# Norms in halves of 256 tokens around a two-block float32 transformer kernel

## The chip, the cores and the metric

The kernel runs on one core of a Trainium2 chip. The metric is the device time of one execution in microseconds, as a median of runs; lower is better. A profile is one execution taken by the hardware profiler. Engines in the profile: PE is TensorE (matmul), PEld its weight loads, DVE is VectorE, ACT is ScalarE, POOL is GpSimd, SP is SyncE, which issues all large transfers.

## The reference

Two transformer blocks run one after the other over 512 tokens of width 1024. What matters here is the order of norms and projections:

```
block 1: u = rmsnorm(h, norm1_w) * (1 + sc1) + sh1;  proj = u @ w_in           # w_in: 28 tiles of 128 columns
         o_hg = hgrn2(...);  o_da = diff_attention(...)
         h = h + g1 * (concat(o_hg, o_da) @ w_out)                             # out1
         u = rmsnorm(h, norm2_w) * (1 + sc2) + sh2                             # norm 1
         h = h + g2 * ((silu(u @ w_gate) * (u @ w_up)) @ w_down)               # ff1, down1
         h = rmsnorm(h, final_norm_w)
block 2: u = rmsnorm(h, ...) * (1 + sc1) + sh1                                 # norm 2
         proj = u @ w_in_2;  kc, vc = compress(k_cmp), compress(v_cmp)         # kc2, qa2, compress, kv2
         sparse attention, stick-breaking attention, gated merge
         h = h + g1 * (merged @ w_out_2)                                       # out2
         u = rmsnorm(h, ...) * (1 + sc2) + sh2                                 # norm 3
         h = h + g2 * ((silu(u @ w_gate_2) * (u @ w_up_2)) @ w_down_2)         # ff2, down2
out = rmsnorm(h, final_norm_w_2)                                               # norm 4
rmsnorm(x, w) = x * rsqrt(mean(x * x) + eps) * w;   mod = silu(c) @ w_ada + b_ada gives the sh, sc, g
compress(k) = gelu((blocks(k) + pos_emb) @ w1) @ w2
```

The final norm of block 1 and norm 2 are computed from one sum over the tokens; a second sum (of raw squares, `ssr`) scales the residual itself later.

## The kernel before

Everything lies transposed: channels on the 128 partitions, tokens along the free axis. `res` holds the residual as 8 tiles of 128 channels x 512 tokens. The weights come as units, one 128-column tile of a weight matrix each (512 KB where all 8 blocks of 128 rows are in it). `plan()` numbers all units of the program in order; `ph.u0` is the first of a phase. SyncE loads a unit into one of two slots of `wraw` as soon as the unit two before it has been split. VectorE splits it (`split`): `wh` is the value rounded for the fast matmul format, `wl` the rest. TensorE then does for each block k three matmuls, `wh` with the high and the low part of the input and `wl` with the high part (`passes`), 24 for a unit, into one bank of 128x512. In-order queues on each engine and counting semaphores set the order: `w_hi` and `w_split` count split units, `unit_done` finished ones, `drain_a` and `drain_v` banks read by ScalarE and VectorE.

A norm goes like this. VectorE adds the bank of each output tile, times its gate, to `res`; ScalarE squares it into `sq`; GpSimd adds up seven of the eight squares in `ssq`. TensorE multiplies `ssq` and the last square with ones to sum over the partitions (`norm`); ScalarE takes the root, VectorE the reciprocal, TensorE spreads it over the partitions with four transposes (`spread`). Then for each of the 8 tiles VectorE makes `tn` (L1705), ScalarE rounds it to `uh` (L1225) and VectorE makes the rest `ul` (L1710). TensorE starts the first two units of the next phase tile by tile as `ul` comes (`passes_both`, L640 to L642). The third unit is split by VectorE only when one of these two is finished. out1a (first half of w_out's rows, 8 units of 4 blocks) leaves tiles 3 to 7 in five banks, and out1 (second half, 8 more units) accumulates onto them.

Behind norm 2, TensorE does kc2 (2 units), then the sums of `ssr` (L991, signals `r_sum`), then the first two units of qa2, the spread of that second root (`r_rstd`), then compress: for n = 0, 1 sixteen matmuls (L1001) and one with `wfin` (L1006), which waits for `c_pos`. GpSimd computes `wfin` from the compress weights in `wpos`, which lies over `ssr`; it waits for `r_sum` ahead of that:

```
g.wait_ge(n_ul, KT * 3)
g.wait_ge(r_sum, 1)
g.wait_ge(c_in, 64)
... wpos[:] = w1c[:, n] * vt2[...]; four folding additions     # L581, L586, each signals c_pos
```

ScalarE drains each of kc2's two banks with four copies (L1446, L1447), and qa2's first unit waits for the first bank (`drain_a`). Norm 4 ends the program: VectorE and ScalarE scale four rows of `outb`, and SyncE stores each.

## Time and profile before

| | us |
|---|---|
| median of 3 runs (lowest, highest) | 1540.92 (1538.4, 1542.06) |
| the profiled execution's own time | 1538.91 |
| its span, first to last instruction | 1537.2 |
| TensorE busy in it | 1463.1 |
| VectorE, ScalarE, GpSimd busy | 986.6, 423.2, 95.5 |

The busy time of TensorE holds each matmul's way through the array, so two neighbours overlap in it; the spacing of starts says how fast a stream runs. "Idle before" in brackets gives the wait ahead of a row and what ended it. The granted clock is a share of full speed.

### The profile page before, as it was taken

How to read it: one execution, taken by the hardware profiler on the slowest of the kernel's cores; microseconds unless marked ns; L12 is line 12 of the kernel's file. 1: busy time of each engine (PE TensorE's matmuls, PEld its weight loads, DVE VectorE, ACT ScalarE, POOL GpSimd, SP SyncE). 2: the span in 40 equal slices, each digit the busy share in tenths (PEclk: the TensorE clock that was granted, in tenths of full speed). 3: DMA queues.
4: the chain of work that ended last, by engine and by line, in shares of the span. 5: the costliest groups of instructions: out<-in, count | busy, mean ns of one | idle time of the engine just before them, and what ended most of it. 6: DMA issues, size and time to landing. Idle time of an engine off the chain costs nothing.

```text
span 1537.2 us, 19550 instructions
## 1 busy us (share of the span) xinstructions
PE 1463.1 (95%) x7186; PEld 1170.1 (76%) x7186; DVE 986.6 (64%) x1727; ACT 423.2 (28%) x901; POOL 95.5 (6%) x75
## 2 busy tenths in 40 slices
PE   3989999889999999998999999999998999999997
PEld 2777876667888888887876666778886888888886
DVE  8789888886767666556556666775546444444343
ACT  5333354432110110003234445531113221221011
POOL 0100000020000000222600000000030000000110
PEclk9999999999999999998999999999998999999999
DMA  9243232344556565543221111113331323233322
GB/s 374 80 156 110 69 138 77 96 144 153 192 195 193 194 195 157 153 126 121 73 69 42 48 50 42 49 49 109 96 110 55 109 84 107 92 99 89 103 86 93
DMA packets 52611, 175.80 MB, mean 114 GB/s; under 512 B 5953, under 2 KB 6337, under 8 KB 52545
## 3 DMA queue, kind: packets, MB, share of 16 engines
q1 hardware_dynamic: 52544, 174.94, 35.1%
q8 instruction: 39, 0.64, 0.2%
q14 instruction: 28, 0.22, 0.0%
HBM read 172.82 MB, written 2.10 MB: 114 GB/s over the span
## 4 chain that ended last, share of the span: by engine, by line
PE 51%; ACT 1%; DVE 1%; issue 0%; ACTq 0%; DVEq 0%
PE bank L628 11%; PE bank L630 11%; PE bank L629 11%; PE bank L1070 8%; PE bank L1089 2%; PE bank L1124 2%; PE bank L1101 2%; PE bank L640 1%; PE bank L641 1%; PE bank L642 1%; PE bank L1001 0%; DVE wl L1611 0%; PE bank L1114 0%; PE bank L1045 0%; PE bank L737 0%
## 5 line engine op out<-in xcount | busy, mean ns | idle before, releaser
L628 PE MATMUL bank<-uh,wh 128*128 128x512 f32 x808 | 316.0, 391 | 6.0 <-DVE wl L1611 4.8
L630 PE MATMUL bank<-uh,wl 128*128 128x512 f32 x808 | 315.1, 390 | 0.0
L629 PE MATMUL bank<-ul,wh 128*128 128x512 f32 x808 | 315.0, 390 | 0.0
L1609 DVE CAST wh<-wraw 128x1024 fp32r<-128x1024 f32 (+1 forms) x235 | 156.2, 665 | 196.8 <-PE bank L630 180.0
L1611 DVE TENSOR_TENSOR wl<-wraw,wh 128x1024 fp32r<-128x1024 f32 (+1 forms) x235 | 275.1, 1171 | 8.1
L628 PEld LDWEIGHTS bank<-uh,wh 128*128 128x128 f32 x808 | 152.1, 188 | 39.0 <-issue 4.9
L630 PEld LDWEIGHTS bank<-uh,wl 128*128 128x128 f32 x808 | 151.9, 188 | 31.9
L629 PEld LDWEIGHTS bank<-ul,wh 128*128 128x128 f32 x808 | 152.1, 188 | 31.4
L628 PE MATMUL bank<-hh,wh 128*128 128x512 f32 x352 | 137.5, 391 | 0.0
L630 PE MATMUL bank<-hh,wl 128*128 128x512 f32 x352 | 137.1, 389 | 0.0
L629 PE MATMUL bank<-hl,wh 128*128 128x512 f32 x352 | 137.0, 389 | 0.0
L1631 DVE CUSTOM_DVE_ANT_0 ada<-ada,scb,vt 128x1024 f32<-128x1024 f32 x80 | 104.8, 1331 | 0.0
L1269 ACT ACTIVATE hh<-hf 128x512 f32 x44 | 27.8, 633 | 246.9 <-DVE hf L1727 246.9
L1727 DVE TENSOR_TENSOR hf<-sg,bank 128x512 f32<-128x512 f32 x44 | 30.2, 688 | 96.8 <-PE bank L630 96.8
L539 POOL TENSOR_TENSOR ssq<-sq 128x512 f32<-128x512 f32 x4 | 7.9, 1978 | 1185.9 <-ACT sq L1208 1185.9
L630 PEld LDWEIGHTS bank<-hh,wl 128*128 128x128 f32 x352 | 66.1, 188 | 13.9
L629 PEld LDWEIGHTS bank<-hl,wh 128*128 128x128 f32 x352 | 66.1, 188 | 13.7
L628 PEld LDWEIGHTS bank<-hh,wh 128*128 128x128 f32 x352 | 66.1, 188 | 13.4
L1070 PE MATMUL bank<-uh,wh 128*128 128x512 f32 x160 | 67.5, 422 | 2.2 <-ACT kdup L1473 2.2
L1070 PE MATMUL bank<-ul,wh 128*128 128x512 f32 x160 | 66.0, 412 | 0.0
L1267 ACT ACTIVATE sg<-bank 128x512 f32<-128x512 f32 x44 | 26.4, 601 | 143.1 <-PE bank L630 137.4
L1070 PE MATMUL bank<-uh,wl 128*128 128x512 f32 x160 | 64.5, 403 | 0.0
(355 smaller groups left out, 2331.6 us busy)
## 6 DMA issues: line engine op xcount, KB each, us to landing
ada<-in_w_ada_dram SPq DMA_DIRECT2D x96, 512.0 KB, 4.6
wraw<-in_w_in_dram SPq DMA_DIRECT2D x61, 512.0 KB, 3.4
wraw<-in_w_ffn_gate_dram SPq DMA_DIRECT2D x44, 512.0 KB, 3.3
wraw<-in_w_ffn_up_dram SPq DMA_DIRECT2D x44, 512.0 KB, 3.3
wraw<-in_w_ffn_down_dram SPq DMA_DIRECT2D x32, 512.0 KB, 3.5
wraw<-in_w_ffn_down_dram SPq DMA_DIRECT2D x16, 384.0 KB, 3.1
wraw<-in_w_out_dram SPq DMA_DIRECT2D x16, 256.0 KB, 2.8
wraw<-in_w_out_dram SPq DMA_DIRECT2D x8, 512.0 KB, 3.4
```

What stands on the lines that cost most here:

```text
L628: nc.tensor.matmul(bank[:], a, rh[:, k0 + k, :], start=(first and k == 0), stop=False)
L629: nc.tensor.matmul(bank[:], a, rl[:, k0 + k, :], start=False, stop=False)
L630: mm = nc.tensor.matmul(bank[:], b, rh[:, k0 + k, :], start=False, stop=(last and k == nk - 1))
L1070: mm = nc.tensor.matmul(B[1][:], (wl if p == 2 else wh)[:, slot, k * P:(k + 1) * P], (ul if p == 1 else uh)[:, k, :], start=(k == 0 and p ...
L1089: mm = nc.tensor.matmul(B[4 + 2 * (m % 2) + ab][:, 0:ZLEN[i]], q[:, i * P:(i + 1) * P], k[:, 0:ZLEN[i]], start=True, stop=True)
L1101: mm = nc.tensor.transpose(B[2 + ab][:, j * P:(j + 1) * P], zt[2 * (m % 3) + ab][:, j * P:(j + 1) * P], ident[:])
L1124: mm = nc.tensor.matmul(B[0][64 * ab:64 * ab + 64, i * P:(i + 1) * P], v, wt2[2 * (m % 2) + ab][:, j * P:(j + 1) * P], start=(first and br ...
L1269: A(hh[:, ds(i, 1), :].rearrange("p a t -> p (a t)"), hf[:, 0], ACT.Copy).then_inc(hh_ok, 1)
L1609: V.tensor_copy(wh[:, slot, 0:n], wraw[:, slot, 0:n]).then_inc(w_hi, 1)
L1611: V.tensor_tensor(wl[:, slot, 0:n], wraw[:, slot, 0:n], wh[:, slot, 0:n].bitcast(F32), ALU.subtract).then_inc(w_split, 1)
L1631: V.tensor_tensor_reduce(ada[:, slot, :], ada[:, slot, :], scb[:, m, :], 1.0, vt[:, t:t + 1], ALU.mult, ALU.add, modt[:, t:t + 1]).then_in ...
L1727: V.tensor_tensor(hf[:, 0], sg[:, 0], B[1][:], ALU.mult).then_inc(h_ok, 1)
```

## The change

The tokens are cut into two halves (`HALVES`) where a norm is near. The last tiles of a projection (from 4 on in out1, 6 and 7 in out2, 7 in down1 and down2) are computed first for 256 tokens, then for the other 256, into two banks; adds, squares, sums, root, spread and the norm's three operations run for each half. VectorE itself adds the last whole square and the first half's squares of norm 1, and one of norm 3. out1 loads its weights as 4 units with two tiles each, and its tiles 4 to 7 no longer accumulate onto out1a's banks; VectorE adds those to `res` by themselves. The two units behind a norm are split into buffers of their own (`XH`), and the third one is rounded by ScalarE (`ahead_cast`) and its rest made by VectorE behind the first tile of the norm (`open_rest`). The modulations of down1 come at other units, the last at the 18th of 24. The sums of `ssr`, with the signal `r_sum`, stand behind qa2's first two units, and the spread that belongs to them behind compress. The final stage scales and stores rows 0, 1 with the first half and rows 2, 3 with the second.

```diff
+        SPLIT_FROM = {1: 4, 2: 7, 3: 6, 4: 7}
+        PARTS = {k: [(t, None) for t in range(m)] + [(t, h) for h in range(2) for t in range(m, KT)]
+                 for k, m in SPLIT_FROM.items()}
+        SQUARED, ADDED, ADDS = {}, {}, {}
+        for k_ in PARTS:
+            for t_, h_ in PARTS[k_]:
+                SQUARED[k_, t_, h_] = len(SQUARED) + 1
+                if 0 < t_ < KT - 1:
+                    ADDED[k_, t_, h_] = len(ADDED) + 1
+            ADDS[k_] = len(ADDED)
+        ADDED_V = {(1, 3, None), (1, 4, 0), (1, 5, 0), (1, 6, 0), (3, 6, 0)}
...
+            def piece(bank, cc, slot, w0, nk, rh, rl, k0, first, last):
+                for k in range(nk):
+                    a = wh[:, slot, (w0 + k) * P:(w0 + k + 1) * P]
+                    b = wl[:, slot, (w0 + k) * P:(w0 + k + 1) * P]
+                    nc.tensor.matmul(bank[:, cc], a, rh[:, k0 + k, cc], start=(first and k == 0), stop=False)
+                    nc.tensor.matmul(bank[:, cc], a, rl[:, k0 + k, cc], start=False, stop=False)
+                    mm = nc.tensor.matmul(bank[:, cc], b, rh[:, k0 + k, cc], start=False, stop=(last and k == nk - 1))
+                return mm
...
+            def behind_norm(ph, nu):
+                hi, lo = XH[ph.name]
+                for h, cc in enumerate(HALVES):
+                    for k in range(KT):
+                        if h == 0 and k == 2:
+                            norm_sums(nu, 1)
+                        if h == 0 and k == 6:
+                            spread_half(nu, 1)
+                        pe.wait_ge(n_ul, N_UL[nu] + KT * h + k + 1)
+                        for c, bank in enumerate(OPEN[ph.name]):
+                            a = hi[:, c, k * P:(k + 1) * P]
+                            b = lo[:, c, k * P:(k + 1) * P]
+                            nc.tensor.matmul(bank[:, cc], a, uh[:, k, cc], start=(k == 0), stop=False)
+                            nc.tensor.matmul(bank[:, cc], a, ul[:, k, cc], start=False, stop=False)
+                            mm = nc.tensor.matmul(bank[:, cc], b, uh[:, k, cc], start=False, stop=(k == KT - 1))
+                            if h and k == KT - 1:
+                                mm.then_inc(unit_done, 1)
...
+                i = ph.iters - 1
+                for t in range(2):
+                    take(ph, i, t)
+                    pe.wait_ge(drain_v, ph.d0 + 2 * i + t - 1)
+                    piece(OUT2_HALF[0][t], HALVES[0], (ph.u0 + t) % 2, 0, KT, rh, rl, 0, True, True).then_inc(tile_ok, 1)
+                piece(OUT2_HALF[1][0], HALVES[1], ph.u0 % 2, 0, NT, rh, rl, 0, True, False)
+                norm_sums(3, 0)
+                piece(OUT2_HALF[1][0], HALVES[1], ph.u0 % 2, NT, NT, rh, rl, NT, False, True).then_inc(unit_done, 1)
+                spread_half(3, 0)
+                piece(OUT2_HALF[1][1], HALVES[1], (ph.u0 + 1) % 2, 0, KT, rh, rl, 0, True, True).then_inc(unit_done, 1)
...
+                slots = [(ph.u0 + 3 + c) % 2 for c in range(3)]
+                take(ph, last, 3)
+                (a0, b0), (a1, b1), (a2, b2) = DOWN
+                bank, other = DOWN_HALF[name]
+                piece(bank, HALVES[0], slots[0], 0, b0 - a0, hh, hl, a0, True, False)
+                piece(other, HALVES[1], slots[0], 0, b0 - a0, hh, hl, a0, True, False).then_inc(unit_done, 1)
+                if tiles_out:
+                    turn_out(KT - 2)
+                take(ph, last, 4)
+                piece(bank, HALVES[0], slots[1], 0, b1 - a1, hh, hl, a1, False, False)
+                take(ph, last, 5)
+                piece(bank, HALVES[0], slots[2], 0, b2 - a2, hh, hl, a2, False, True).then_inc(tile_ok, 1)
+                piece(other, HALVES[1], slots[1], 0, NT, hh, hl, a1, False, False)
+                norm_sums(4 if tiles_out else 2, 0)
+                piece(other, HALVES[1], slots[1], NT, NT, hh, hl, a1 + NT, False, False).then_inc(unit_done, 1)
+                if tiles_out:
+                    turn_last(0)
+                else:
+                    spread_half(2, 0)
+                piece(other, HALVES[1], slots[2], 0, b2 - a2, hh, hl, a2, False, True).then_inc(unit_done, 1)
...
+            def norm_sums(k, h):
+                pe.wait_ge(ssq_ok, added(k, KT - 2, h))
+                if h:
+                    pe.wait_ge(sq_ok, squared(k, KT - 1, h))
+                for j in (2 * h, 2 * h + 1):
+                    nc.tensor.matmul(SUMS[k][:, j:j + 1], ssq[:, j * P:(j + 1) * P], ones[:, 0:1], start=(j == 2 * h),
                                      stop=False, skip_group_check=True)
-                pe.wait_ge(sq_ok, KT * k)
-                for j in range(NT):
-                    mm = nc.tensor.matmul(B[4][:, j:j + 1], sq[:, 1, j * P:(j + 1) * P], ones[:, 0:1], start=False,
-                                          stop=(j == NT - 1), skip_group_check=True)
+                pe.wait_ge(sq_ok, squared(k, KT - 1, h))
+                for j in (2 * h, 2 * h + 1):
+                    mm = nc.tensor.matmul(SUMS[k][:, j:j + 1], sq[:, 1, j * P:(j + 1) * P], ones[:, 0:1], start=False,
+                                          stop=(j == 2 * h + 1), skip_group_check=True)
                 mm.then_inc(n_sum, 1)
+            def spread_half(k, h):
+                pe.wait_ge(n_col, 2 * (k - 1) + h + 1)
+                for j in (2 * h, 2 * h + 1):
+                    mm = nc.tensor.transpose(SPREAD[k][h][:, j * P:(j + 1) * P], rcol[:, j:j + 1].broadcast_to([P, P]),
+                                             ident[:])
+                mm.then_inc(n_rstd, 1)
...
+            for h, cc in enumerate(HALVES):
+                for t in range(4, KT):
+                    slot, w0 = take(ph, 0, t // 2), NT * (t % 2)
+                    if h:
+                        pe.wait_ge(part_ok, t - 3)
+                    else:
+                        pe.wait_ge(drain_v, ph.d0 + t - 3)
+                    mm = piece(OUT1_HALF[h][t - 4], cc, slot, w0, NT, mixh, mixl, NT, True, True)
+                    mm.then_inc(unit_done if h and t % 2 else tile_ok, 1)
+                    if h and t == 4:
+                        norm_sums(1, 0)
+                    if h and t == 5:
+                        spread_half(1, 0)
+            ffn("ff1", 1, H1)
             down("down1", 0)
-            norm(2)
-            spread(B[7], rcol, n_col, 2, n_rstd)
-            simple("kc2", uh, ul, 2 * KT)
+            ph = PH["kc2"]
+            take(ph, 0, 1)
+            pe.wait_ge(drain_a, ph.a0)
+            behind_norm(ph, 2)
...
+            simple("qa2", uh, ul, part=(0, 1))
             pe.wait_ge(ssr_ok, 7)
             for j in range(NT):
                 mm = nc.tensor.matmul(B[6][:, j:j + 1], ssr[:, j * P:(j + 1) * P], ones[:, 0:1], start=(j == 0),
                                       stop=(j == NT - 1), skip_group_check=True)
             mm.then_inc(r_sum, 1)
-            simple("qa2", uh, ul, part=(0, 1))
-            spread(B[6], rcolr, r_col, 1, r_rstd)
 
...
+            spread(B[6], rcolr, r_col, 1, r_rstd)
...
+            def ahead_cast(ph):
+                u = ph.u0 + 2
+                act.wait_ge(w_in[u % 2], 16 * (u // 2 + 1 - FRONT // 2))
+                act.wait_ge(unit_done, u - 3 + U1)
+                act.wait_ge(w_split, u)
+                A(wh[:, u % 2, :], wraw[:, u % 2, :], ACT.Copy).then_inc(w_hi, 1)
...
+            def through_norm(nu, name, late, shift, bias=epst, scale=None, then=None):
+                ph = {1: PH["ff1"], 2: PH["kc2"], 3: PH["ff2"]}[nu]
+                norm_std(nu, 0, bias)
+                ahead_cast(ph)
                 for t in range(KT):
-                    act.wait_ge(n_t, KT * (nu - 1) + t + 1)
-                    A(uh[:, t, :], tn[:, t % 4], ACT.Identity, bias=shift[:, t:t + 1]).then_inc(n_uh, 1)
+                    norm_u(nu, shift, t, 0)
+                    if t >= 1 and t - 1 < len(late):
+                        part_square(name, nu, late[t - 1], 1, scale)
+                    if t == 3 + len(late):
+                        norm_std(nu, 1, bias)
+                for t in range(KT):
+                    norm_u(nu, shift, t, 1)
...
+            def split_open(ph, c):
+                u = ph.u0 + c
+                slot, (hi, lo) = u % 2, XH[ph.name]
+                v.wait_ge(w_in[slot], 16 * (u // 2 + 1 - FRONT // 2))
+                V.tensor_copy(hi[:, c, :], wraw[:, slot, :]).then_inc(w_hi, 1)
+                v.wait_ge(w_hi, u + 1)
+                V.tensor_tensor(lo[:, c, :], wraw[:, slot, :], hi[:, c, :].bitcast(F32),
+                                ALU.subtract).then_inc(w_split, 1)
...
+            def open_rest(ph):
+                u = ph.u0 + 2
+                v.wait_ge(w_hi, u + 1)
+                V.tensor_tensor(wl[:, u % 2, :], wraw[:, u % 2, :], wh[:, u % 2, :].bitcast(F32),
+                                ALU.subtract).then_inc(w_split, 1)
...
+            def through_norm(nu, shift, late):
+                ph = {1: PH["ff1"], 2: PH["kc2"], 3: PH["ff2"]}[nu]
+                for h in range(2):
+                    for t in range(KT + 1):
+                        if t < KT:
+                            norm_in(nu, t, h)
+                        if t:
+                            norm_low(nu, shift, t - 1, h)
+                        if h == 0 and t == 1:
+                            open_rest(ph)
+                        if h == 0 and 1 <= t <= len(late):
+                            late[t - 1]()
+                        if h == 0 and t == len(late) + 4:
+                            norm_rstd(nu, 1)
...
+            def add_out1a(t):
+                v.wait_ge(unit_done, PH["out1a"].u0 + t + 1 + U1)
+                V.scalar_tensor_tensor(res[:, t, :], (B[1] if t < 3 else OUT1_BANKS[t])[:], mod1[:, 16 + t:17 + t], res[:, t, :],
+                                       op0=ALU.mult, op1=ALU.add).then_inc(drain_v if t < 3 else part_ok, 1)
+            def add_out1(t, h=None):
+                n = {None: t, 0: t, 1: t + 4}[h]
+                ph = PH["out1"]
+                if h == 0:
+                    v.wait_ge(part_ok, t - 3)
+                if t % 2 and h != 0:
+                    v.wait_ge(unit_done, ph.u0 + t // 2 + 1 + U1)
+                else:
+                    v.wait_ge(tile_ok, {0: 1, 2: 2, 4: 3, 5: 4, 6: 5, 7: 6, 8: 7, 10: 8}[n])
+                add_part(OUT1_BANKS[t] if h is None else OUT1_HALF[h][t - 4], t, h, mod1[:, 16:24])
...
+            ph, fu = PH["out1"], PH["ff1"]
+            split(ph.u0 + 1, (ph.u0 + 1) % 2)
+            add_out1(0)
+            for t in (4, 5):
+                add_out1a(t)
+            add_out1(1)
+            split(ph.u0 + 2, ph.u0 % 2)
+            for t in (6, 7):
+                add_out1a(t)
+            add_out1(2)
+            split(ph.u0 + 3, (ph.u0 + 1) % 2)
+            add_out1(3)
+            add_square(1, 3)
+            split_open(fu, 0)
+            for t in range(4, KT):
+                add_out1(t, 0)
+                if t > 4:
+                    add_square(1, t - 1, 0)
+            add_out1(4, 1)
+            v.wait_ge(mod_done, 40)
+            gains(1, mod1, vt1, NORM_B, 32)
+            split_open(fu, 1)
+            norm_rstd(1, 0)
+            through_norm(1, mod1[:, 24:32], [lambda t=t: add_out1(t, 1) for t in (5, 6, 7)])
```

## Rows read from the trace of the kernel before

**Rows 1.** the page, busy us, share of the span and instructions of TensorE.
```profile
PE 1463.1 (95%) x7186; PEld 1170.1 (76%) x7186; DVE 986.6 (64%) x1727; ACT 423.2 (28%) x901; POOL 95.5 (6%) x75
```

**Rows 2.** stretches around the norms: length, busy (x) of PE, PEld, DVE, ACT, POOL; PEclk, DMA, GB/s.
```profile
311.00:334.40 23.40, 22.50 (x96) 17.79 (x96) 20.87 (x33) 4.72 (x8) 8.16 (x6) 1.00 0.58 180
334.40:341.30 6.90, 2.74 (x21) 2.27 (x20) 5.30 (x9) 2.37 (x5) 1.20 (x1) 0.81 0.48 152
341.30:354.30 13.00, 12.95 (x48) 10.39 (x48) 8.97 (x14) 7.15 (x9) 0.00 (x0) 0.84 0.00 0
354.30:362.40 8.10, 5.98 (x26) 4.48 (x25) 7.23 (x11) 1.37 (x3) 0.00 (x0) 1.00 0.58 190
705.20:713.20 8.00, 3.66 (x22) 3.10 (x20) 6.32 (x10) 2.89 (x5) 1.63 (x1) 0.64 0.42 130
713.20:726.20 13.00, 13.00 (x48) 10.56 (x49) 8.87 (x14) 4.80 (x7) 0.00 (x0) 0.83 0.43 154
1152.30:1160.00 7.70, 3.71 (x21) 3.11 (x19) 5.00 (x8) 2.27 (x4) 0.00 (x0) 0.64 0.26 85
1160.00:1173.20 13.20, 13.15 (x48) 10.55 (x48) 8.96 (x14) 6.08 (x8) 0.00 (x0) 0.82 0.00 0
```

**Rows 3.** TensorE, groups by line (busy, mean ns), then its timeline (start, duration).
```profile
L817 PE MATMUL bank<-ql,kl 128*128 128x128 f32 x224 | 30.7, 281 | 2.9 <-DVE kl L1899 2.8
...
195.36 1.05 PE L817 MATMUL bank<-ql,kl 128*128 128x128 f32 x8
```

**Rows 4.** VectorE, groups by line, then one row of its timeline.
```profile
L1611 DVE TENSOR_TENSOR wl<-wraw,wh 128x1024 fp32r<-128x1024 f32 x203 | 251.9, 1241 | 7.0
...
L1631 DVE CUSTOM_DVE_ANT_0 ada<-ada,scb,vt 128x1024 f32<-128x1024 f32 x80 | 104.8, 1331 | 0.0
...
L1705 DVE SCALAR_TENSOR_TENSOR tn<-res,gain,bank 128x512 f32<-128x512 f32 x24 | 17.5, 741 | 3.3 <-PE bank L745 2.1 <-issue 1.3
...
L1899 DVE TENSOR_TENSOR kl<-p,xx 128x256 f32<-128x256 f32 x28 | 11.7, 417 | 0.0
...
318.74 2.31 DVE L1631 CUSTOM_DVE_ANT_0 ada<-ada,scb,vt 128x1024 f32<-128x1024 f32 x1
```

**Rows 5.** ScalarE, timeline behind norm 1 and behind kc2.
```profile
349.24 1.28 ACT L1434 ACT_TABLE_LOAD   x1
350.54 1.06 ACT L1434 ACTIVATE scb<-scb 128x1024 f32<-128x1024 f32 x1
...
725.75 0.59 ACT L1446 ACTIVATE kds<-bank 64x512 f32<-64x512 f32 x1 [4.71 <-PE bank L642]
```

**Rows 6.** GpSimd, timeline of the compress weights.
```profile
727.31 3.93 POOL L581 TENSOR_TENSOR wpos<-w1c,vt 128x2048 f32<-128x2048 f32 x1 [18.16 <-PE bank L991]
...
737.16 0.46 POOL L586 TENSOR_TENSOR wfin<-wpos 128x128 f32<-128x128 f32 x1
...
747.18 0.46 POOL L586 TENSOR_TENSOR wfin<-wpos 128x128 f32<-128x128 f32 x1
```

**Rows 7.** TensorE, timeline from kc2 to qa2's third unit.
```profile
726.23 0.94 PE L991 MATMUL bank<-ones,ssr 128*128 128x1 f32 x8
728.29 0.47 PE L628 MATMUL bank<-uh,wh 128*128 128x512 f32 x1 [1.12 <-ACT kds L1447]
...
735.18 0.50 PE L628 MATMUL bank<-uh,wh 128*128 128x512 f32 x1 [1.20 <-DVE wl L1611]
...
741.23 3.71 PE L1001 MATMUL bank<-kds,w1c 128*128 128x62 f32 x32
...
748.56 0.32 PE L1006 MATMUL bank<-ones,wfin 128*128 128x1 f32 x2
```

**Rows 8.** timeline of the last tile and of the tail.
```profile
1520.22 0.39 PE L629 MATMUL bank<-hl,wh 128*128 128x512 f32 x1
...
1525.89 0.39 PE L630 MATMUL bank<-hh,wl 128*128 128x512 f32 x1
...
1531.58 0.35 ACT L1593 ACTIVATE outb<-bank,tiny 128x128 f32<-128x128 f32 x1
```

423 lines of the change are left out of this document (230 added, 193 removed).

## The prediction

> **What bounds the kernel now.** I read the page's busy shares first, then the waits of TensorE, then its timeline wherever it idles, and last the stretches by engine. TensorE is busy 95% of the span [rows 1], so time can be won only where it idles or crawls. Three such places are alike: the norms behind out1, down1 and out2. TensorE issues its last projection, then for 6.9, 8.0 and 7.7 us does only the sums and the spread of 1/std, and then its 48 matmuls of the first two tiles take 13.0, 13.0 and 13.2 us instead of 48 x 0.227 = 10.9, since part of them runs at the lower clock level: the granted clock averages 0.84, 0.83 and 0.82 [rows 2]; the 0.227 is the spacing of the matmuls at 1520.22 and 1525.89, 25 places apart [rows 8]. Behind the first norm the third tile also waits for VectorE. These are what the change aims at. The fourth place is the tail, 11.3 us from the last matmul to the end of the span [rows 8]. A fifth row matters for what the change moves: GpSimd's work on the compress weights, which today is just hidden [rows 6, 7].
>
> **The price of halves.** A pair of weight load and 256-column matmul is not in this trace. The nearest row is L817: eight pairs, each a 128x128 load and a matmul of 128 columns in plain float32, take 1.05 us, the last one's own 0.281 included, so (1.05 - 0.281)/7 = 0.110 apart [rows 3]. From above: a whole one of 512 columns costs 0.227; if what is not columns (0.227 - 512/2.4 GHz = 0.014) is fixed, a half costs 0.107 + 0.014 = 0.120. I take 0.117, so a whole in two halves costs 0.007 more; ends 0.110 and 0.120, and 0.125 if loads interfere. VectorE: a TENSOR_TENSOR falls from 1.241 us at 1024 columns to 0.417 at 256, 0.275 per 256 columns [rows 4]. So the norm's instruction of 0.741 (spaced 0.66, each starts 0.08 before its forerunner ends) becomes 0.47, spaced 0.41 (an estimate, from these rows; 0.33 if it scaled fully, 0.45 with more overhead). 32 of them take 13.1 us instead of 16 x 0.66 = 10.6. TensorE consumes a half tile for two weight tiles in 6 x 0.117 = 0.70 while VectorE makes it in 0.82: behind each norm VectorE sets the pace.
>
> Row L817 says 0.110 per pair. The Trainium skill (TensorE: Matmul & The Clock Gate, "Back-to-back issue gap") gives 262 cycles for N = 256, that is 109 ns when warm. It gives 216 ns for N = 512, where this trace has 227, so I don't take it; by it the halves would win about 3 us over my sum, which speaks for rival 2.
>
> **out1 and norm 1.** VectorE is busy 20.9 of 23.4 us there already [rows 2]. Added on it: four adds of out1a's tiles 4 to 7 into res (they used to stay in PSUM) 4 x 0.66 = 2.6; eight half adds for four whole +0.6; one whole and three half additions of squares +1.6. Four wide splits for eight narrow ones give back 1.0. Going through its new order from 311.0 (first split 0.8 longer, then splits 3 x 1.9, three modulations 3.8, adds 7.9, squares 2.3 with the wait for ScalarE, both opening splits 3.8, the small ones 0.5), the reciprocal of the first half comes at about 335.8. Sums and spread for that half cost 0.9 more, then 13.1 for the halves, 1.15 for the rest of the third tile, 1.2 for three late half adds, 0.9 for the second reciprocal and waits where a half begins: 353.0. TensorE meanwhile stands about 3 us before the first sums, and that costs nothing, since VectorE is the late one. Collisions with GpSimd: a modulation of 1.33 took 2.31 beside a GpSimd add [rows 4]; I take 1.2, between 0 and 2.5. So the last low half is there at 354.2. Next is late: ScalarE loads its table (1.28), does the Silu of the second condition vector (1.06) and the first Silu of the FFN (some 0.6, as its copies) [rows 5], and the third tile's matmuls wait for that: 356.7. Before, TensorE issued 26 matmuls in the 8.1 us up to 362.4, which are 5.9 us of work [rows 2]: 2.2 lost by waits for the split tiles, 1.7 of it ahead of the third tile (start 356.0) and the rest a tile later, so its effective start is 356.8. Change: 0 (from -2 to +2).
>
> The row at 318.74 shows the slowing [rows 4]. The skill (SBUF — State Buffer, "Who interferes with whom") says VectorE with two SBUF inputs and GpSimd hold a shared port pair exclusively, for whole instructions. By it the squares moved from GpSimd to VectorE save VectorE up to 1 us each time; that is inside my bounds.
>
> **down1 and norm 2, up to compress.** I count from the start of down1's last tile: 705.22 - 66 x 0.227 = 690.2. Its first half is complete after 90 halves, 10.5. Behind it VectorE adds (0.2 later, 0.47), ScalarE squares, TensorE has 12 halves as cover and sums at 12.0 to 12.9; std and reciprocal come under the next 12 halves; spread at 14.5; first norm instruction at 14.8; ScalarE's cast of the third tile (1.04) delays the first high half by 0.3; then 13.1 + 1.15 + 0.4 (late add) + 1.3 (reciprocal; the second half's spread stands behind k = 5 on TensorE and is about 0.6 late): last low half 30.8, kc2 complete at 31.6. Before it was 726.2 - 690.2 = 36.0. qa2's first unit waits, as before [rows 7], for the four copies of kc2's first bank, 4 x 0.59 [rows 5], with the raw square now ahead of them: starts at 34.0 instead of 38.1. A gain of 4.1.
>
> Then comes the step that I think decides. GpSimd multiplies and folds the compress weights: it starts when r_sum has been signalled (727.31, right behind L991 at 726.23) and ends its first result at 737.6 (737.16 and its 0.46), its second at 747.6 [rows 6, 7]: 11.4 and 21.4 us after the sums begin. TensorE waits for these (c_pos) inside compress. Before, qa2's two units stood between the r_sum matmuls and compress, and the second wait was met with one microsecond to spare (748.56 against 747.64). The change puts the r_sum matmuls behind qa2's units, right ahead of compress. GpSimd's wait on r_sum is unchanged, and so is its chain. Now nothing but 2 x 3.6 us of compress matmuls lies beside 20.3 us of GpSimd. With R the start of the r_sum matmuls: matmuls of n = 0 until R + 4.6, wait until R + 11.4 (6.8 us idle), n = 1 until about R + 15 to 18.5, wait until R + 21.4. Without the waits it is R + 8.7: a stall of 12.8 (12 to 13.5; GpSimd's second round had VectorE beside it and took as long as the first, so it won't shorten much). Behind such a gap TensorE starts at its lower level, and the norms lost 2.1 us by that; I add 2.0. Queued behind the wait on TensorE: the spread for raw_rows and qa2's last two units; VectorE waits with them for c_h.
> R = 34.0 + 2 x 5.44 = 44.9; the second c_h at 66.4, spread 0.4: qa2's third unit at 66.8. Before: 748.8 - 690.2 = 58.6, its stall of 1.2 [rows 7] included. With the slow clock: a loss of 10.2; rounded with VectorE's uncertain spacing 10.4. Tables on GpSimd shift too, but stand to TensorE as before, counted from R.
>
> **out2 and norm 3.** From the start of tile 6, 1152.3 - 2 x 5.44 = 1141.4. Both first halves are done at 5.7; VectorE comes to them at 4.8 behind two splits, adds and squares until 6.9; sums at 7.1 to 8.1; spread 9.8; first norm instruction 10.1; then 0.6 for the cast, 13.1, 1.15, 0.8 (two late adds) and 0.9: 26.6; matmuls end at 27.4, before 31.8. The third tile is rounded already, so it starts at about 28.1, behind table load and Silu; before, it waited for the split as behind norm 1, 1.7 us, 33.5. A gain of 5.4, with 1 us either way.
>
> **down2 and the tail.** 66 wholes in halves +0.5; sums and transposes of the first half now lie in TensorE's stream, with the turn of tile 6 before them, +1.6. The tail behind 1525.9, in which ScalarE scales the last row until 1531.9 [rows 8], shortens: add -0.27, square and the copy behind it -0.8, two rows instead of four to scale -1.0, half the bytes to store perhaps -0.3. Sum -0.3, taken as 0 (-1 to +1.5).
>
> **Sum.** 0 + 10.4 - 5.4 + 0 = +5.0 on the profiled execution's 1538.9 (span 1537.2 and 1.7 around it): 1543.9. That execution lies 2.0 below the median of the runs; on the median it is 1545.9, predicted 1546.
>
> **Rivals.**
> 1. The stall at compress isn't there, because GpSimd gets done ahead of TensorE after all. Without the 12.8 and the 2.0 the sum is -9.8: 1531. For it: the norms do shorten in the way the rows say. Against it: the wait on r_sum still stands in GpSimd's queue and its rows have no slack. It decides from the point where GpSimd's start no longer follows qa2. Chance 0.10; the other side.
> 2. Halves cost 0.110 and norm 1 wins its 2 us: some 320 halves are not under VectorE's pace, 320 x 0.007 = 2.2, together -4.2: 1541.7, no change. For it row L817, against it that the type there is another. 0.16.
> 3. The lower clock level comes on also in the halved norms, as TensorE waits about 1 us again and again for VectorE. A half tile then takes 6 x 0.213 = 1.28 and not 0.70, above VectorE's 0.82; for 4 us at each norm that is about 1.5 us, three times: +4.5, 1550.4. For it: the granted clock of 0.64 in two of the gaps [rows 2]. Against: the new gaps are far shorter. 0.12.
> Forecast as summed: 0.62.
>
> **Numbers.** A change of 0.2% (3.1 us) is about what can be told from none. The forecast's own spread is 3.5 us, 1542.5 to 1549.5. Slower: nearly all of the forecast and rival 3, 0.72. Same: rival 2 and the low edge of the forecast, 0.18. Faster: 0.10. The range, with rival 2's lower values and rival 3: 1539.5 to 1551.5.
>
> **What would show it.** Right: in the waits of TensorE, the matmul with wfin (L1006 before) waits for GpSimd twice, about 6.8 and 3 to 6 us; kc2's matmuls end about 4 us earlier against down1; ff2's third tile starts without waiting for wl. 256-column matmuls 0.110 to 0.125 apart. The norm's VectorE instructions spaced 0.41. Wrong: no wait for GpSimd in compress; halves above 0.15 apart; a clock below 1.0 through the halved norms; norm 1 more than 2 us off either way.

## The result

The changed kernel takes 1547.58 us in the median (1546.08 to 1550.08, 5 runs), the kernel before 1540.92 (1538.4 to 1542.06, 5 runs beside them): the ratio is 1.0047, with a 95% interval of 1.0037 to 1.0058. Predicted were 1546 and slower. The profiled execution has a span of 1543.7 us, against 1537.2; it was the fastest of the five, with a time of 1546.08 us, so 2.4 us of its time lie outside the span, where the kernel before has 1.7.

The page's busy line of the changed kernel, beside [rows 1]: TensorE is busy 7.2 us longer and idle no longer in sum than before (73.4 us, before 74.1). The new waits behind norm 2 are not to be seen here, since the norms have given up as much idle time elsewhere, and slow matmuls count as busy. The stretches between fixed points show the loss.

```profile
PE 1470.3 (95%) x7558; PEld 1194.7 (77%) x7558; DVE 993.3 (64%) x1786; ACT 408.3 (26%) x919; POOL 89.6 (6%) x74
```

I laid the two traces side by side at seven fixed points of TensorE's timeline. Each number is the length of one stretch in us:

| stretch | before | after | difference | predicted |
|---|---|---|---|---|
| start to the end of a wait for the attention's weights (287.89, 289.23) | 287.9 | 289.2 | +1.3 | 0 |
| to the start of down1's last tile | 402.4 | 405.5 | +3.1 | 0 |
| to qa2's third unit | 58.5 | 66.7 | +8.2 | +8.2 |
| to out2's tile 6 | 392.7 | 392.0 | -0.7 | +2.0 |
| to the third unit of the second FFN | 33.5 | 28.0 | -5.5 | -5.4 |
| to down2's last tile | 336.1 | 336.1 | 0 | 0 |
| to the end of the span | 26.2 | 26.2 | 0 | 0 |

The first row has nothing to do with the change: that point lay between 287.9 and 289.8 in the profiled executions of all kernels of this study, before any changed instruction. Each stretch is read from one execution of each kernel, so a difference of one or two us can also be scatter.

The wait that I had named as the deciding one. TensorE's waits in the changed kernel (us in total, times, longest), and then its timeline (start, duration) from the r_sum matmuls (now L1122, before L991) to qa2's third unit, which answers to [rows 7]:

```profile
PE bank L1135 <- POOL wfin L636: 6.5, 2, 5.2
```
```profile
741.54 0.95 PE L1122 MATMUL bank<-ones,ssr 128*128 128x1 f32 x8
742.35 3.79 PE L1130 MATMUL bank<-kds,w1c 128*128 128x62 f32 x32
751.38 0.59 PE L1135 MATMUL bank<-ones,wfin 128*128 128x1 f32 x2 [5.24 <-POOL wfin L636]
751.83 7.07 PE L1130 MATMUL bank<-kds,w1c 128*128 128x62 f32 x32
760.18 0.59 PE L1135 MATMUL bank<-ones,wfin 128*128 128x1 f32 x2 [1.28 <-POOL wfin L636]
760.63 1.09 PE L859 MATMUL bank<-ident,tiny 128*128 128x128 f32 x4
761.37 0.78 PE L678 MATMUL bank<-uh,wh 128*128 128x512 f32 x1
```

The same 32 matmuls of 62 columns take 3.79 us ahead of the first wait and 7.07 behind it. The granted clock was 1.00 from 742.35 to 747.00 and 0.50 from 751.83 to 760.00, the lower of the two levels, so it fell in the gap; and the second round was slow enough to hide most of the second wait. GpSimd's timeline of the same stretch, which answers to [rows 6]:

```profile
742.62 3.61 POOL L631 TENSOR_TENSOR wpos<-w1c,vt 128x2048 f32<-128x2048 f32 x1 [14.01 <-PE bank L1122]
746.31 4.48 POOL L636 TENSOR_TENSOR wpos<-wpos 128x1024 f32<-128x1024 f32 x3
750.87 0.46 POOL L636 TENSOR_TENSOR wfin<-wpos 128x128 f32<-128x128 f32 x1
...
759.67 0.45 POOL L636 TENSOR_TENSOR wfin<-wpos 128x128 f32<-128x128 f32 x1
```

Its round takes 8.7 us, where [rows 6] show 10.3 and 10.0: VectorE has nothing to do meanwhile. Its first instruction has 14.01 us of idle time before it, and in brackets stands what it waited for: TensorE's L1122.

The stretches of the changed kernel around the norms (length, busy (x) of PE, PEld, DVE, ACT, POOL, then PEclk, DMA, GB/s), beside [rows 2]:

```profile
312.00:336.66 24.66, 19.18 (x110) 16.37 (x108) 23.70 (x35) 4.99 (x10) 4.43 (x2) 1.00 0.54 170
336.66:344.80 8.14, 8.14 (x43) 8.14 (x43) 5.77 (x11) 2.60 (x6) 0.72 (x1) 0.58 0.20 67
344.80:361.35 16.55, 14.13 (x113) 13.47 (x111) 15.04 (x37) 11.17 (x21) 1.69 (x2) 1.00 0.12 36
...
741.50:761.37 19.87, 13.35 (x81) 12.95 (x81) 1.15 (x6) 2.46 (x5) 17.81 (x13) 0.71 0.00 0
...
1160.00:1181.39 21.39, 20.19 (x161) 19.34 (x161) 17.61 (x41) 12.57 (x25) 0.80 (x1) 1.00 0.24 75
```

Ahead of the first norm VectorE is busy 23.70 of 24.66 us, and the 8 us behind run at the lower level (0.58). At the third norm nothing of the kind is seen: the granted clock is 1.00 throughout, against 0.64 and 0.82 in [rows 2].

### The profile page after: what moved, and what is told of

Its sections match the earlier page's. It is cut to its first block, busy times and chain, and to the rows that moved or that the text cites. A ratio compares the mean times of both kernels' runs of the same rounds, so it can differ in the third digit from the quotient of the medians.

```text
span 1543.7 us, 20402 instructions
## 1 busy us (share of the span) xinstructions
PE 1470.3 (95%) x7558; PEld 1194.7 (77%) x7558; DVE 993.3 (64%) x1786; ACT 408.3 (26%) x919; POOL 89.6 (6%) x74
## 4 chain that ended last, share of the span: by engine, by line
PE 85%; DVE 8%; ACT 3%; issue 2%; POOL 1%; DMA 0%; DVEq 0%; SPq 0%; ACTq 0%; POOLq 0%
PE bank L678 18%; PE bank L680 18%; PE bank L679 18%; PE bank L1200 8%; PE bank L1219 2%; PE bank L1254 2%; PE bank L931 2%; PE bank L1231 2%; PE bank L903 1%; PE bank L905 1%; PE bank L904 1%; PE bank L1041 1%; DVE ada L1795 1%; PE bank L688 1%; PE bank L876 1%
## 5 line engine op out<-in xcount | busy, mean ns | idle before, releaser
L1759 DVE CAST wh<-wraw 128x1024 fp32r<-128x1024 f32 (+1 forms) x222 | 148.3, 668 | 183.1 <-PE bank L680 170.3
L1761 DVE TENSOR_TENSOR wl<-wraw,wh 128x1024 fp32r<-128x1024 f32 (+1 forms) x222 | 259.3, 1168 | 7.6
L678 PE MATMUL bank<-hh,wh 128*128 128x512 f32 x308 | 120.3, 391 | 0.0
L680 PE MATMUL bank<-hh,wl 128*128 128x512 f32 x308 | 119.9, 389 | 0.0
L679 PE MATMUL bank<-hl,wh 128*128 128x512 f32 x308 | 119.9, 389 | 0.0
L1423 ACT ACTIVATE hh<-hf 128x512 f32 (+1 forms) x44 | 27.8, 632 | 240.9 <-DVE hf L1930 240.9
L680 PEld LDWEIGHTS bank<-hh,wl 128*128 128x128 f32 x308 | 57.8, 188 | 12.0
L679 PEld LDWEIGHTS bank<-hl,wh 128*128 128x128 f32 x308 | 57.8, 188 | 11.9
L678 PEld LDWEIGHTS bank<-hh,wh 128*128 128x128 f32 x308 | 57.8, 188 | 11.9
## 6 DMA issues: line engine op xcount, KB each, us to landing
fraw<-in_w_in_dram SPq DMA_DIRECT2D x6, 512.0 KB, 14.8
```

Source lines behind the costliest of these rows:

```text
L678: nc.tensor.matmul(bank[:], a, rh[:, k0 + k, :], start=(first and k == 0), stop=False)
L679: nc.tensor.matmul(bank[:], a, rl[:, k0 + k, :], start=False, stop=False)
L680: mm = nc.tensor.matmul(bank[:], b, rh[:, k0 + k, :], start=False, stop=(last and k == nk - 1))
L1759: V.tensor_copy(wh[:, slot, 0:n], wraw[:, slot, 0:n]).then_inc(w_hi, 1)
L1761: V.tensor_tensor(wl[:, slot, 0:n], wraw[:, slot, 0:n], wh[:, slot, 0:n].bitcast(F32), ALU.subtract).then_inc(w_split, 1)
```

## The experiments

All were timed against the kernel before on the same chip; it had medians of 1540.3, 1541.0 and 1540.9 us in the three groups of runs. Line numbers of the variants are shifted against the changed kernel's where lines came or went.

**1. The order of r_sum alone, taken back.**

```diff
+            (r_sum matmuls, signal r_sum)
             simple("qa2", uh, ul, part=(0, 1))
-            (r_sum matmuls, signal r_sum)
             (compress)
```

> The changed kernel with one block moved back: the four r_sum matmuls stand again right behind kc2's tiles, ahead of the first two units of qa2. Theory (the wait for GpSimd inside compress is the loss): GpSimd starts its two rounds of 8.7 us at about 729.7 instead of 742.6 and is done at 738.4 and 747.2, and TensorE comes to the two matmuls with wfin at about 745.3 and 749, so it waits for neither; the 6.5 us of waits, the slow matmuls of the second round and the slow clock behind it go, 12.6 us in all: 1547.6 - 12.6 = 1535.0, and 1533 to 1537. Rival (what comes behind compress, the rows rescaled by VectorE or the copies of ScalarE, holds qa2's third unit anyway): the wait shows up under another name, 1545 to 1548.

Measured: 1534.62 us (1533.65 to 1537.81), ratio 0.9963 (0.9950 to 0.9975). TensorE's timeline at the second wait:

```profile
749.36 0.38 PE L1135 MATMUL bank<-ones,wfin 128*128 128x1 f32 x2 [0.25 <-POOL wfin L636]
749.61 0.63 PE L859 MATMUL bank<-ident,tiny 128*128 128x128 f32 x4
750.00 0.47 PE L678 MATMUL bank<-uh,wh 128*128 128x512 f32 x1
```

6.5 us of waits became 0.25, the third unit starts at 750.00 and not at 761.37, and the time falls by 13.0 us in the median, against 12.6 expected. (The two profiled spans lie 10.6 apart: that of the changed kernel was the fastest of its five executions, that of experiment 1 the second slowest.) The rival falls: nothing behind compress held it. GpSimd began at 729.93 as expected; its first round took 10.6 us, not 8.7, since VectorE was busy beside it, and that still fitted.

**2. The same order put into the kernel before, all norms whole.**

```diff
-            (r_sum matmuls)
             simple("qa2", uh, ul, part=(0, 1))
-            spread(B[6], rcolr, r_col, 1, r_rstd)
+            (r_sum matmuls)
             (compress)
+            spread(B[6], rcolr, r_col, 1, r_rstd)
```

> The kernel before with the reverse edit alone: the r_sum matmuls behind qa2's first two units, and with them, as in the changed kernel, the root on ScalarE, the reciprocal on VectorE, the spread behind compress and the first two rescaled rows. All norms whole. Theory: from r_sum to qa2's third unit 19.8 us as in the changed kernel, where the kernel before has r_sum at 727.3 and the third unit at 748.7: r_sum at 739.2, third unit at 759.0, plus 1.1 of slow clock: 1540.9 + 11.4 = 1552.3, and 1550 to 1554. Rival (the loss is of the halves and not of this order): 1540 to 1543.

Measured: 1555.14 us (1552.77 to 1555.55), ratio 1.0088 (1.0075 to 1.0101), 14.8 over the kernel before. Its timeline:

```profile
742.37 0.95 PE L992 MATMUL bank<-ones,ssr 128*128 128x1 f32 x8
743.18 3.79 PE L1000 MATMUL bank<-kds,w1c 128*128 128x62 f32 x32
752.21 0.59 PE L1005 MATMUL bank<-ones,wfin 128*128 128x1 f32 x2 [5.23 <-POOL wfin L586]
752.66 7.07 PE L1000 MATMUL bank<-kds,w1c 128*128 128x62 f32 x32
761.01 0.58 PE L1005 MATMUL bank<-ones,wfin 128*128 128x1 f32 x2 [1.29 <-POOL wfin L586]
761.46 1.10 PE L745 MATMUL bank<-ident,tiny 128*128 128x128 f32 x4
762.20 0.78 PE L628 MATMUL bank<-uh,wh 128*128 128x512 f32 x1
```

The pattern is the changed kernel's row by row, 19.8 us from r_sum to the third unit, with no norm halved. The order alone makes a kernel slower than the whole change does. It came out 2.8 above my number and above my range. In its profiled execution the stretch from down1's last tile to qa2's third unit is 10.4 us longer than in the kernel before, as worked out (10.3). What is over lies elsewhere: 1.6 us ahead of everything changed, 1.4 in the first norm, untouched, and 3.1 between qa2's third unit and out2's tile 6, where the matmuls ran at the lower clock level longer: about 1.5 right behind the compress gap (1.1 expected) and 1.5 behind the 64 matmuls of 32 columns that follow later (L1045). Stretches there, for the kernel before, the changed one and this one (columns as above):

```profile
774.00:778.00 4.00, 4.00 (x30) 3.35 (x29) 2.63 (x4) 0.00 (x0) 0.00 (x0) 0.70 0.01 2
```
```profile
790.00:794.00 4.00, 4.00 (x19) 3.33 (x18) 3.90 (x5) 1.06 (x1) 0.00 (x0) 1.00 0.00 0
```
```profile
792.00:796.00 4.00, 4.00 (x10) 3.09 (x10) 3.90 (x5) 1.06 (x1) 0.00 (x0) 0.50 0.01 2
```

Which of this comes in every execution and which is scatter of single ones, no run shows.

**3 and 4. The first norm and out1 whole again**, on the changed kernel, and on experiment 1's.

```diff
-        Phase("out1", 1, 4, 0, 8, 4)
+        Phase("out1", 1, 8, 0, 8)
-        SPLIT_FROM = {1: 4, 2: 7, 3: 6, 4: 7}
+        SPLIT_FROM = {1: 8, 2: 7, 3: 6, 4: 7}
...
+                        if nu == 1:
+                            passes_both((B[0], B[1]), slots, uh, ul)
```

> The changed kernel with out1 and the first norm as in the kernel before: eight half units of out1, out1a's tiles 4 to 7 left in PSUM, all squares of this norm added by GpSimd, one reciprocal and one spread, whole instructions, the first two tiles of the FFN in the ring's slots. The norms behind down1, out2 and down2 stay in halves. Theory from the two traces (the first norm in halves lost 3.2 us: the third unit starts 75.4 us behind a fixed gap in TensorE's work and not 72.1): 1547.6 - 3.2 = 1544.4. My prediction (net 0 here): 1547.6. Below 1543 the halves of out1 cost more than the traces show.

> Both edits together: r_sum ahead of qa2 and the first norm whole. If the two losses are independent: 1547.6 - 12.6 - 3.2 = 1531.8. If the time won at the first norm is given back before compress (by the weights' loads or by a wait for VectorE), 1535, as with r_sum alone.

Measured: 1545.32 us (1542.02 to 1546.61), ratio 1.0031 (1.0020 to 1.0042); and 1531.35 us (1526.87 to 1532.72), ratio 0.9932 (0.9919 to 0.9945). The first of these came 0.9 above the expected 1544.4. So halving the first norm costs 2.3 us by the first pair of medians and 3.3 by the second; the intervals of the first pair overlap, those of the second don't. From the attention's wait to the third unit of the FFN the traces have 72.1 us in the changed kernel, 72.2 in experiment 1, and 69.0 and 68.3 with the norm whole (68.1 in the kernel before). Over all profiled executions of the study this stretch took 70.9 to 73.8 us with the first norm in halves and 68.1 to 69.7 with it whole. The two losses add up as expected in experiment 4 (1531.8). The fourth kernel, that of experiment 4, is 9 us under the kernel before: the change without its first norm and with r_sum where it was. Only experiment 6, a variant of it, is as fast.

Not all of that cost lies in the norm. With the first norm in halves, the tail behind the start of down2's last tile takes 26.2 us (26.5 in experiment 9), and with it whole but the rest changed 25.5, although the tail's program is the same; the last store is issued 0.36 us behind the end of the issue before it, and not 0.04. And outside the span lie 1.7 to 1.9 us of the time in every execution of the kernels with the first norm whole, but 1.7 to 4.0, 2.4 in the median, in those with it in halves. So about 1.3 us of the 2.3 to 3.3 come at the end of the program or outside the span; what causes them no run shows.

**5. Squares of the first norm back on GpSimd**, on experiment 1's kernel.

```diff
-        ADDED_V = {(1, 3, None), (1, 4, 0), (1, 5, 0), (1, 6, 0), (3, 6, 0)}
+        ADDED_V = {(3, 6, 0)}
```

> The changed kernel with r_sum ahead of qa2 (1534.6), and with the first norm's four additions of squares that VectorE had taken (one of 512 columns, three of 256) given back to GpSimd; all else in halves as it is. Theory (the first norm loses because VectorE is the late engine ahead of its first reciprocal): these four take 0.69 + 3 x 0.41 = 1.9 us of VectorE; GpSimd's own last half addition of 0.7 to 0.85 then stands in the chain instead of 0.41, so about 1 us is won: 1533.6. Rival (GpSimd's additions slow VectorE's instructions beside them as much as they relieve it, by 1 us for each whole one): 1534.6 to 1536.

Measured: 1536.85 us (1535.13 to 1540.74), ratio 0.9975 (0.9964 to 0.9987). The theory missed: slower by 2.2 and not faster by 1, and a little above the rival's range too. The intervals of this run and of experiment 1 overlap, so the size is uncertain; in the traces the norm takes 73.8 us and 72.2. The first sums of the norm wait for GpSimd, longer than they waited for VectorE (2.81):

```profile
337.63 0.60 PE L839 MATMUL bank<-ones,ssq 128*128 128x1 f32 x4 [3.56 <-POOL ssq L589]
```

So taking these additions to VectorE seems to have paid in the change, although VectorE is the busy engine there.

**6. The spread of the second half behind k = 3**, on the fourth kernel, at the norm behind down1.

```diff
-                        if h == 0 and k == 6:
+                        if h == 0 and k == (4 if nu == 2 else 6):
                             spread_half(nu, 1)
```

> The kernel with r_sum ahead of qa2 and the first norm whole (1531.35), and the spread of the second half's 1/std behind k = 3 of the first half's tiles instead of behind k = 5, at the norm behind down1 alone. Theory: the reciprocal is there 3.6 us before TensorE gets to the spread, VectorE stands 1.77 us for it, and that time goes straight through kc2, qa2 and GpSimd's start: 1531.35 - 1.7 = 1529.7. Rival (the next late thing, ScalarE's last half squares or the copies of kc2, holds qa2 at its old time): 1531.3.

Measured: 1531.15 us (1528.2 to 1531.71), ratio 0.9932 (0.9919 to 0.9946): nothing won. Yet VectorE no longer waits for the spread. Its timeline in the fourth kernel, then in this one:

```profile
717.91 0.48 DVE L1893 SCALAR_TENSOR_TENSOR tn<-res,gain,bank 128x256 f32<-128x256 f32 x1 [1.77 <-PE bank L863]
```
```profile
716.39 0.47 DVE L1893 SCALAR_TENSOR_TENSOR tn<-res,gain,bank 128x256 f32<-128x256 f32 x1
```

kc2 ended 1.5 us sooner, and qa2's first two units started at 726.63 instead of 728.14. But their 48 matmuls took 12.3 us and not 10.8, as the granted clock was lower there. From the start of down1's last tile to qa2's third unit 54.4 us are left of the fourth kernel's 55.3. Why the median shows nothing of these 0.9 isn't shown; in this trace the first norm, which the edit leaves as it was, took 1.4 us longer. Stretches of the fourth kernel, then of this one (columns as above):

```profile
712.00:716.00 4.00, 4.00 (x25) 4.00 (x24) 3.79 (x11) 2.46 (x6) 0.00 (x0) 0.60 0.02 4
...
728.00:732.00 4.00, 3.85 (x17) 3.25 (x18) 3.50 (x3) 2.38 (x5) 3.92 (x2) 1.00 0.43 137
```
```profile
712.00:716.00 4.00, 4.00 (x35) 4.00 (x36) 3.81 (x12) 2.70 (x6) 0.00 (x0) 1.00 0.03 6
...
728.00:732.00 4.00, 4.00 (x15) 3.20 (x14) 2.02 (x1) 0.90 (x2) 3.92 (x2) 0.73 0.33 124
```

**7. The third norm and out2 whole as well**, on the fourth kernel.

```diff
-        Phase("out2", 4, 2, 0, 2, 2)
+        Phase("out2", 4, 2, 0, 2)
-        SPLIT_FROM = {1: 8, 2: 7, 3: 6, 4: 7}
+        SPLIT_FROM = {1: 8, 2: 7, 3: 8, 4: 7}
```

> The kernel with r_sum ahead of qa2 and the first norm whole (1531.35), and the norm behind out2 whole as well, with out2 and the first FFN tiles as in the kernel before. What is left in halves is the norm behind down1 and the tail. By the prediction's term for the third norm (5.4): 1536.8. Then the norm behind down1 is left with 1540.3 - 1536.8 = 3.5, beside my 4.1. If out2's halves are worth less than the traces say (a wait that moves on to the FFN), 1533 to 1535.

Measured: 1536.54 us (1534.97 to 1537.34), ratio 0.9971 (0.9959 to 0.9982). The expected 1536.8 holds and the rival's 1533 to 1535 falls. The third norm's halves are worth 5.2 us by the medians, against 5.4 in the sum, and what is left of the change, the norm behind down1 with the tail, 4.4.

**8. The spread behind k = 3 at the first two norms**, on experiment 1's kernel; the edit is that of 6 with `k == (6 if nu == 3 else 4)`.

> The changed kernel with r_sum ahead of qa2 (1534.6; first norm in halves) and the spread of the second half's 1/std behind k = 3 instead of k = 5 at the norms behind out1 and down1. Theory: VectorE starts its second half 1.4 us sooner at the first norm and 1.7 us sooner at the second: 1531.5. Rival (at the first norm ScalarE's table load and the two Silus hold the third unit whatever VectorE does): only the second norm's part, 1532.9.

Measured: 1533.16 us (1531.74 to 1533.86), ratio 0.9951 (0.9937 to 0.9965), nearer to the rival. In the trace the first norm is 1.2 us shorter (71.0 instead of 72.2), so the theory of that part holds. The median of the spans fell by 2.2 us (1532.4 to 1530.2), more than that of the times (1.5), since 3.0 us of the time lie outside the span here. The time stays 2.0 us above experiment 6's, which has the first norm whole, but the span only 0.8.

**9. The first two additions of squares on VectorE too**, on experiment 1's kernel.

```diff
-        ADDED_V = {(1, 3, None), ...
+        ADDED_V = {(1, 1, None), (1, 2, None), (1, 3, None), ...
```

> The changed kernel with r_sum ahead of qa2 (1534.6), and of the first norm's squares also the first two whole additions on VectorE, so that GpSimd adds none beside out1's splits and modulations. Theory (a GpSimd addition of 2.2 us beside a modulation costs VectorE 1.03 us, twice, in the traces of before, after and this parent): VectorE pays 2 x 0.66 = 1.3 for the additions and gets 2 x 1.03 = 2.1 back, the two modulations take 1.28 and not 2.32: 0.7 won, 1533.9. Rival (the modulations are slow for another reason, the landing of their rows for one): they stay at 2.3 and the time is 1534.6 + 1.3 = 1535.9.

Measured: 1535.26 us (1532.62 to 1537.08), ratio 0.9961 (0.9946 to 0.9975). The modulations do get fast. VectorE in the changed kernel, then here:

```profile
321.54 2.32 DVE L1795 CUSTOM_DVE_ANT_0 ada<-ada,scb,vt 128x1024 f32<-128x1024 f32 x1
...
327.62 2.31 DVE L1795 CUSTOM_DVE_ANT_0 ada<-ada,scb,vt 128x1024 f32<-128x1024 f32 x1
```
```profile
321.04 1.28 DVE L1795 CUSTOM_DVE_ANT_0 ada<-ada,scb,vt 128x1024 f32<-128x1024 f32 x1
...
326.68 1.28 DVE L1795 CUSTOM_DVE_ANT_0 ada<-ada,scb,vt 128x1024 f32<-128x1024 f32 x1
```

So the price of a collision, 1.03 us, is shown: with GpSimd quiet it is gone. The time can't be told from the parent's, and in the trace the norm is only 0.2 us shorter (72.0).

**10 and 11. Experiments 6 and 8 once more**, unchanged, for the clock.

> The kernel of run e6_spread_earlier once more, for its clock. There kc2 ended 2.0 us sooner (counted with the 0.5 us that it began later), and qa2's first two units then ran 12.3 us and not 10.75, since the granted clock behind the 2.5 us gap ahead of them was 0.85 and 0.73 in two stretches of 4 us. If the lower clock level there is bound to the shorter way to the gap, it comes again and the time is 1531.2. If it falls by chance behind one or the other gap, the 48 matmuls take 10.75 here and the span is about 1528.

> The kernel of run e8_spread_earlier_halves once more, for the same question: its profiled execution showed a clock of 1.00 from 700 to 752 us and a span of 1528.7, while the median of its runs was 1533.2, 2.8 more than that span and the 1.7 us around it. If the lower level comes behind one of the gaps in most executions, this profile shows it in qa2 or in the first half of the norm, 1.5 us longer, and a span of 1530 to 1532.

Measured: 1531.53 us (1529.49 to 1532.21) and 1533.34 us (1531.41 to 1534.98); profiled spans 1527.7 and 1531.0. Both lie where they were expected: about 1528 if the level falls by chance, and 1530 to 1532 if it comes behind one of the gaps in most executions. Experiment 10 ran qa2's first 48 matmuls in 10.8 us at a clock of 1.00 and had the lower level (0.64) in the half ahead; 11 had it in qa2 (0.66 from 728 to 732), where 8 had it in neither. The same program thus meets the low level behind one gap, the other, or none; the repetitions ran on another chip than the first runs, so chance and chip aren't told apart. In experiment 10 the slow half was not free: kc2 ended 32.8 us behind the start of down1's last tile, in experiment 6 31.7. VectorE waited 0.44 us for the second spread, and TensorE, behind by then, ran kc2's second half without a pause to its end. So both came to qa2's third unit after the same 54.4 us. Experiment 10's stretch that answers to the third of 6's pair:

```profile
712.00:716.00 4.00, 4.00 (x23) 4.00 (x24) 3.38 (x9) 2.02 (x5) 0.00 (x0) 0.64 0.00 0
```

## Why the prediction was right

**The deciding step was right, and is shown.** "Now nothing but 2 x 3.6 us of compress matmuls lies beside 20.3 us of GpSimd": experiments 1 and 2 move r_sum, one way and the other (2 with the root, reciprocal and spread that belong to it), and the time goes by -13.0 and +14.8. I had it at 10.4 with the norm's gain of 4.1 taken off, so 14.5 by itself. The waits were forecast as 6.8 and 3 to 6 and came as 5.24 and 1.28. Two sizes were off against each other: a round of GpSimd took 8.7 us, not 10.0 (I had said that the second round wouldn't shorten much), which takes 2.1 off the way from r_sum to the third unit (19.8, not 21.9); and the second norm had given only 2.1 of my 4.1 at qa2's first unit. So the third unit came at 66.7, forecast 66.8: the mechanism was right, the agreement to 0.1 us is luck.

**Norm 2.** kc2 ended 33.5 us behind the start of down1's last tile, not 31.6 (36.0 before). The failed step is "the second half's spread stands behind k = 5 on TensorE and is about 0.6 late". It was 1.88 late, as the 24 halves between the second sums and it were 0.188 apart in the mean, partly at the lower level. That is 1.3 of the 1.9 us. Another 0.25 is a slip of adding: the terms that I give for the last low half make 31.05, not 30.8. In experiment 6, with the spread behind k = 3 and the clock at 1.00, kc2 did end at 31.7. VectorE stood still for the spread:

```profile
720.32 0.87 DVE L1881 SCALAR_TENSOR_TENSOR tn<-res,gain,bank 128x256 f32<-128x256 f32 x2 [1.88 <-PE bank L851]
```

**Norm 1: "Change: 0 (from -2 to +2)" was wrong.** It costs 2.3 to 3.3 us by experiments 3 and 4, and 3.2 by the trace once the stretch's late units are counted as I had. Two steps failed. The reciprocal of the first half was to come at 335.8; with the 1.3 us that this execution was late from the start that is 337.1, and it came at 339.44. Collisions with GpSimd make 1.4 of these 2.3: they came to 2.6 (twice 1.03, and 0.57 on the split at 337.71), and I had put 1.2. The other 0.9 I can't give to one row. And "sums and spread for that half cost 0.9 more" left out what stands ahead of the spread on TensorE: twelve matmuls of out1, at 0.21 apart instead of 0.12, since TensorE had waited 2.81 us for VectorE and the clock had fallen.

```profile
337.71 1.80 DVE L1778 TENSOR_TENSOR x1l<-wraw,x1h 128x1024 fp32r<-128x1024 f32 x1
339.44 0.15 DVE L1874 RECIPROCAL tiny<-tiny 128x2 f32<-128x2 f32 x1
341.74 0.87 DVE L1881 SCALAR_TENSOR_TENSOR tn<-res,gain,bank 128x256 f32<-128x256 f32 x2 [2.15 <-issue]
```
```profile
336.66 0.94 PE L839 MATMUL bank<-ones,ssq 128*128 128x1 f32 x4 [2.81 <-DVE ssq L1869]
337.46 0.99 PE L843 MATMUL bank<-ones,sq 128*128 128x1 f32 x4
338.31 0.56 PE L688 MATMUL bank<-mixh,wh 128*128 128x256 f32 x1
...
341.02 0.63 PE L851 MATMUL bank<-ident,tiny 128*128 128x128 f32 x2
```

I had written that TensorE standing 3 us ahead of the first sums "costs nothing, since VectorE is the late one". It cost the clock of what followed, and the spread is in that. That makes 1.4 more. From 341.74 on my steps held in sum: 19.6 us to the third unit, forecast 20.0.

The runs show a part of this only. Experiment 8 puts the second spread's place at 1.2 us in the trace. Experiment 9 takes the two collisions away, and its first reciprocal does come 1.45 us sooner; but the third unit came only 0.2 sooner, since the 24 halves ahead of its second spread were 0.188 apart, and 0.123 in the changed kernel. The low level ate what VectorE had won. And by the times, some 1.3 of the 2.3 to 3.3 us lie behind the norm, at the end of the program or outside the span (experiments 3 and 4), which no term of mine held. How much of the rest is VectorE's added work alone (four adds of 0.66 that PSUM used to take, eight half adds) was not tried by itself.

**Prices.** A pair of load and 256-column matmul takes 0.120 us, over the 102 in a row behind 694.68, at the upper end of my 0.110 to 0.120; the 109 ns that follow from the 262 cycles of the Trainium skill (TensorE: Matmul & The Clock Gate, "Back-to-back issue gap") are not reached here, so rival 2 falls by its price as well as by its time. VectorE's instruction of 256 columns takes 0.48 and is spaced 0.39, forecast 0.47 and 0.41:

```profile
694.68 0.28 PE L688 MATMUL bank<-hh,wh 128*128 128x256 f32 x1
694.80 0.28 PE L689 MATMUL bank<-hl,wh 128*128 128x256 f32 x1
```

**Norm 3** gave 5.5 us in the trace and 5.2 in experiment 7, forecast 5.4. The third unit of the second FFN starts behind ScalarE's Silu, no longer behind a split, as said:

```profile
1181.39 0.50 PE L678 MATMUL bank<-uh,wh 128*128 128x512 f32 x1 [0.35 <-ACT sg L1421]
```

**The tail** gave nothing, as forecast: 17.3 us and not 14.9 from the start of the last tile to its last matmul, and as much less behind it. With the first norm whole the same tail gives 0.7 (experiments 3 and 4). **The slow clock behind the compress gap** cost 1.1 us in qa2's next 48 matmuls (12.0 for 10.9), not 2.0, and the whole stretch to out2 was even 0.7 shorter than before. The traces say where: behind the 64 matmuls of 32 columns the kernel before met the lower level (0.70 in the row under experiment 2) and spent 7.2 us on the next 24 matmuls, while the changed kernel kept 1.00 and spent 5.6. Why the level differs there stays open.

**The rivals.** 1 (no stall) is refuted by the waits and by experiment 1, which is what it describes: there the time is 1534.6. The rival had 1531, as it too put the first norm at nothing. Rival 3 was right in part: the lower level did come on in halved norms, at the first and the second, not at the third. In the changed kernel it cost by the spread that waits behind the slow halves, not by the halves themselves, as I had priced it; in experiment 10 the two together cost 1.1 us at norm 2.

The sum came out 1.6 us short of the median. By the table, +3.1 at the first norm and +1.3 of scatter were missed, and 2.7 behind compress was charged too much (0.9 of it the slow clock in qa2, 1.6 the lower level that the kernel before met later and the changed one didn't). The sum also kept 1.7 us outside the span, where the changed kernel has 2.2 to 2.8. That the total came so near is thus partly luck: misses of 1 to 3 us of both signs stand in it.

## What to carry to other kernels

When a producer's signal is moved behind other work, look at who starts by it and how long that one needs: here four tiny matmuls moved back by 11 us cost 13 us, because the 17 us and more of GpSimd's work waited for them and had been hidden with one us to spare. A small instruction that frees another engine (a spread, a sum) must stand where its operand is ready, not behind the last full block of matmuls, and least of all behind a gap, where that block ran partly at half clock in 8 of the 11 profiled executions with the norm behind down1 in halves. Splitting into halves pays where the splitting engine is idle (out2, down1) and lost here where it is the busy one (out1), though a part of that loss lies at the end of the program and is unexplained.
